# A second copy of the forget sums, batched routing, and the distance table copied from device memory

## What is computed

```python
mod = silu(c) @ w_ada                                   # six rows: shift, gain and gate, twice
h = rms_norm(x) * gain + shift
proj = h @ w_in                                         # q, k, v of "a" and of "b"; 8 forget logits a token
log_f = log_sigmoid(f_logit + b_forget)
# attention a, 8 heads of 64:  s = q.k/8 + cum[q] - cum[k], cum = cumsum(log_f); causal; softmax; @ v
# attention b, 8 heads of 64:  s = q.k/8 + rel_bias[bucket(q - k)]; causal; softmax; @ v
x = x + gate * rms_norm(concat(y_a, y_b) @ w_out)
h = rms_norm(x) * gain_f + shift_f
logits = h @ w_router + b_router                        # 32 experts
top_v, top_i = top_k(logits, 4); gates = softmax(top_v)
# every token goes to its 4 experts (swiglu, 1024 -> 2048 -> 1024), summed with the gates
```

## Time and profile before

| | |
|---|---|
| median of 3 runs | 2198.4 us (2195.64 to 2199.47) |
| the profiled execution | 2199.45 us, span 2197.5 us, mean granted clock 0.957 |
| busy: PE, weight loads, DVE, ACT, POOL | 92%, 60%, 36%, 32%, 12% of the span |
| DMA | 608.93 MB, 277 GB/s on average |
| chain that ended last | PE 70%, DMA 10%, SP queue 5%, issue 5%, DVE 5%, ACT 3% |

### The profile page before, as it was taken

One profiled execution on the slowest core, in us unless ns is written; L12 is line 12 of the kernel. 1 busy time (PEld: TensorE's weight loads), 2 busy tenths in 40 slices (PEclk: granted clock), 3 DMA queues, 4 the chain that ended last, 5 costly groups with the idle time before them and its releaser, 6 DMA issues.

```text
span 2197.5 us, 30287 instructions
## 1 busy us (share of the span) xinstructions
PE 2017.9 (92%) x11629; PEld 1311.4 (60%) x11630; DVE 800.1 (36%) x1351; ACT 704.7 (32%) x1092; POOL 260.6 (12%) x243
## 2 busy tenths in 40 slices
PE   5998699999999999999999979997999799997998
PEld 2785333333333333333333368986998699987996
DVE  2443411211111111111211166516675475246663
ACT  2434211112111221122222145523554355415543
POOL 3040000000000000000100002000242020000340
PEclk7889699999999999999999989998999899998999
DMA  9786599999896999799999855434555354453553
GB/s 356 154 285 268 232 389 418 417 416 417 325 416 284 417 416 418 324 418 416 418 418 417 362 178 178 147 118 153 170 177 191 122 192 135 135 185 122 184 182 115
DMA packets 203793, 608.93 MB, mean 277 GB/s; under 512 B 10946, under 2 KB 115542, under 8 KB 167312
## 3 DMA queue, kind: packets, MB, share of 16 engines
q1 hardware_dynamic: 197600, 585.40, 69.8%
q0 software_dynamic: 5776, 21.35, 3.4%
q10 hardware_dynamic: 328, 0.95, 0.1%
HBM read 604.51 MB, written 9.24 MB: 279 GB/s over the span
## 4 chain that ended last, share of the span: by engine, by line
PE 70%; DMA 10%; SPq 5%; issue 5%; DVE 5%; ACT 3%; DVEq 0%; ACTq 0%
PE bank L738 33%; PE bank L995 15%; PE bank L1024 9%; DMA ring<-in_w_gate_up 7%; PE bank L1088 3%; PE bank L955 2%; SPq L619 2%; SPq L622 2%; DMA ring<-in_w_in 2%; PE bank L968 1%; PE bank L988 1%; DMA ring<-in_w_ada 1%; ACT probs L1579 1%; DVE split L1416 1%; PE bank L788 1%
## 5 line engine op out<-in xcount | busy, mean ns | idle before, releaser
L995 PE MATMUL bank<-ring,qkv 128*64 128x512 f32 x2240 | 496.5, 596 | 13.4 <-DMA ring<-in_w_gate_up 13.3
L738 PE MATMUL bank<-hT_hi,split 128*128 128x256 f32 x2432 | 443.8, 285 | 5.4 <-DVE hT_lo L1424 4.0
L738 PEld LDWEIGHTS bank<-hT_hi,split 128*128 128x128 f32 x2432 | 383.4, 194 | 8.2 <-issue 6.9
L1416 DVE TENSOR_TENSOR split<-ring,split 128x2048 fp32r<-128x2048 f32 x120 | 283.8, 2367 | 265.1 <-ACT split L1737 264.9
L1737 ACT ACTIVATE split<-ring 128x2048 fp32r<-128x2048 f32 x120 | 229.6, 1913 | 415.9 <-PE bank L738 333.7
L995 PEld LDWEIGHTS bank<-ring,qkv 128*64 128x64 f32 x2240 | 155.2, 137 | 337.7 <-issue 294.4
L738 PE MATMUL bank<-hT_lo,split 128*128 128x256 f32 x1216 | 346.3, 285 | 0.0
L1024 PE MATMUL bank<-ring,qkv 128*64 128x512 f32 x1120 | 255.8, 598 | 25.7 <-ACT qkv L1698 23.5
L738 PEld LDWEIGHTS bank<-hT_lo,split 128*128 128x128 f32 x1216 | 235.8, 194 | 0.0
L1394 DVE SCALAR_TENSOR_TENSOR out_halves<-bank,probs,out_halves 64x512 fp32r<-64x512 f32 x70 | 52.5, 750 | 395.6 <-ACT out_halves L1720 395.1
L1384 DVE TENSOR_SCALAR qkv<-bank 128x512 f32<-128x512 f32 x35 | 24.2, 692 | 423.0 <-PE bank L995 423.0
(11 more groups left out here) (281 smaller groups left out, 2306.3 us busy)
## 6 DMA issues: line engine op xcount, KB each, us to landing
ring<-in_w_gate_up SPq DMA_DIRECT2D x256, 1024.0 KB, 17.0
ring<-in_w_down SPq DMA_DIRECT2D x150, 1024.0 KB, 15.8
ring<-in_w_in SPq DMA_DIRECT2D x58, 1024.0 KB, 5.4
ring<-in_w_up SPq DMA_DIRECT2D x44, 1024.0 KB, 5.1
ring<-in_w_ada SPq DMA_DIRECT2D x24, 1024.0 KB, 10.1
ring<-in_w_out SPq DMA_DIRECT2D x12, 1024.0 KB, 6.1
ring<-in_w_branch SPq DMA_DIRECT2D x12, 1024.0 KB, 5.1
neighbours<-rpb_copies POOLq DMA_DIRECT2D x32, 128.0 KB, 9.5
```

Source lines behind the costliest of these rows:

```text
L738: last = pe.matmul(out, a[a_half], b[b_half], start=start and i == 0, stop=stop and i == 2)
L995: last = pe.matmul(hidden[q][CAP * j:CAP * j + CAP, :], xgT[:, k % 4, k // 4, :], unit_at(k)[:, c:c + 512], start=False, stop=(k == KC - 1))
L1416: dve.tensor_tensor(low, unit_at(u % RING_L), high.bitcast(F32), ALU.subtract).then_inc(low_done, 1)
```

## The change

- **Forget sums.** `FOX_ROWS` is 104: the constant `fox_table` has its ones and minus ones also in rows 64 on and 96 on. `wfdup` has 64 columns and TensorE runs the product twice, to partitions 0 to 63 and 64 to 127 of the bank. The vector and scalar operations cover 104 partitions, and the product with the sums and the memset are done for rows 32 to 39 and 96 to 103. The odd head's bias takes rows 64 to 103. The wait on `odd_scores` is gone.
- **Homes.** `bada`, `trow` and `crow` move from `side` to `mixT_t`, `wfdup` to `probs_t`; two small loads of `b_forget` are added.
- **Distance table.** POOL writes the 8 rows once (`distance_rows`), waits, copies that 128 times from device memory to `distances`, and waits.
- **Routing.** Equalities, sums and gate products cover both token tiles in one instruction each; the counts are read from PSUM directly; the gates' arithmetic moves behind the evacuation of `turned`, with a bank of its own (`turned_gates`) for its transposes; the zeroing of `y_halves` moves ahead of the logits.

```diff
@@ scores
-                            if o:
-
-                                last.then_inc(odd_scores, 1)
-                                pe.wait_ge(odd_scores, tt * PAIRS + h // 2 + 1)
-                            last = extra(b, tt, h)
+                            last = extra(b, tt, h, o)
@@ TensorE, forget sums and bias
             for k in range(KC):
-                last = pe.matmul(b[0:40, 0:T], wfdup[:, k, :], hT[:, k, :], start=(k == 0), stop=(k == KC - 1))
+                for o in (0, DH):
+                    last = pe.matmul(b[o:o + DH, 0:T], wfdup[:, k, :], hT[:, k, :], start=(k == 0), stop=(k == KC - 1))
...
-            def fox_bias(b, tt, h):
-                return pe.matmul(b[:, 0:T], fcum[:, tt * P:tt * P + P], fox_rhs[:, h, :], start=False, stop=True)
+            def fox_bias(b, tt, h, o):
+                return pe.matmul(b[:, 0:T], fcum[o:o + 40, tt * P:tt * P + P], fox_rhs[o:o + 40, h, :], start=False,
+                                 stop=True)
@@ VectorE, forget sums
-            own(dve.tensor_tensor(fox_rhs[32:40], fox_rhs[32:40], fcum[32:40].unsqueeze(1).broadcast_to([8, HEADS, T]),
-                                  ALU.mult))
-            dve.memset(fcum[32:40, :], 1.0).then_inc(fox_ready, 1)
+            for group in fox_groups[1::2]:
+                own(dve.tensor_tensor(fox_rhs[group], fox_rhs[group],
+                                      fcum[group].unsqueeze(1).broadcast_to([HEADS, HEADS, T]), ALU.mult))
+            for group in fox_groups[1::2]:
+                last = dve.memset(fcum[group, :], 1.0)
+            last.then_inc(fox_ready, 1)
@@ VectorE, routing
-            for tt in range(TT):
-                for k in range(TOPK):
-                    last = dve.tensor_scalar(equal4[:, k, :], experts, bestf[:, tt, k:k + 1], None, ALU.is_equal)
-                own(last)
-                last = dve.tensor_reduce(chosen[:, tt, :], equal4.rearrange("p k e -> p e k"), AX_X, ALU.add)
...
+            own(dve.tensor_tensor(equal4, experts.unsqueeze(1).unsqueeze(1).broadcast_to([P, TT, TOPK, EXPERTS]),
+                                  over_experts(bestf[:, :, 0:TOPK]), ALU.is_equal))
+            dve.tensor_reduce(chosen, equal4.rearrange("p t k e -> p t e k"), AX_X, ALU.add).then_inc(route_ready, 1)
...
-            dve.tensor_scalar(posT, bank("turned")[0:EXPERTS, 0:T], starts, None, ALU.add)
-            leave(dve.tensor_copy(gateT, bank("turned")[0:EXPERTS, T:2 * T]), "turned")
+            leave(dve.tensor_scalar(posT, bank("turned")[0:EXPERTS, 0:T], starts, None, ALU.add), "turned")
+            dve.wait_ge(gates_exp, 1)
+            own(dve.reciprocal(gsum, gsum))
+            own(dve.tensor_tensor(gate4, gate4, gsum.unsqueeze(2).broadcast_to([P, TT, TOPK]), ALU.mult))
+            own(dve.tensor_tensor(equalg, equal4, over_experts(gate4), ALU.mult))
+            dve.tensor_reduce(gates_te, equalg.rearrange("p t k e -> p t e k"), AX_X, ALU.add).then_inc(route_ready, 1)
@@ POOL
-            pool.dma_start(distances.rearrange("q h d -> h q d"), trow.unsqueeze(1).broadcast_to([HEADS, P, 2 * T]))\
-                .then_inc(table_out, 16)
+            pool.dma_start(distance_rows, trow).then_inc(table_out, 16)
             pool.wait_ge(table_out, 16)
+            pool.dma_start(distances.rearrange("q h d -> q (h d)"),
+                           distance_rows.rearrange("h d -> (h d)").partition_broadcast(P)).then_inc(table_out, 16)
+            pool.wait_ge(table_out, 32)
```

More of the change, by code:

```diff
@@ L34 @@
 QK_SCALE = DH ** -0.5
+FOX_ROWS = DH + 40
 RING = 6
@@ L123, in shape_tables @@
     table = np.concatenate([np.asarray(a, np.float32) for a in parts.values()], 1)
[L124 to L127, removed]
+    fox = np.zeros((FOX_ROWS, HEADS, T), np.float32)
+    for base in (0, DH):
+        for h in range(HEADS):
+            fox[base + h, h], fox[base + 32 + h, h] = 1.0, -1.0
+    return np.ascontiguousarray(table), at, fox.reshape(FOX_ROWS, HEADS * T)
 class Plan:
@@ L223, in plan_first @@
         p.tile(f"g{j}")
-    for n in ("logits", "places", "counts", "ends", "turned", "list", "spread0", "spread1"):
+    for n in ("logits", "places", "counts", "ends", "turned", "list", "turned_gates", "spread0", "spread1"):
         p.tile(n)
@@ L933, in _ @@
                            stop=True))
-            read("turned")
+            pe.wait_ge(route_ready, 5)
+            b = take("turned_gates")
+            for tt in range(TT):
+                last = pe.transpose(b[0:EXPERTS, tt * P:tt * P + P], gates_te[:, tt, :], ident)
+            tile(last)
+            read("turned", "turned_gates")
             for tt in range(TT):
@@ L1247, in _ @@
             dve.wait_ge(cleared, 1)
-            for a in (0, 32):
-                last = dve.tensor_copy(wfdup[:, :, a:a + HEADS], wf)
+            for group in fox_groups[:2]:
+                last = dve.tensor_copy(wfdup[:, :, group], wf)
             last.then_inc(forget_in, 1)
@@ L1299, in _ @@
             await_own("logits")
-            for tt in range(TT):
-                own(dve.max(best[:, tt, :], logits[:, tt, :]))
-                own(dve.max_index(picked[:, 8 * tt:8 * tt + 8], best[:, tt, :], logits[:, tt, :]))
+            dve.max(best[:, 0, :], logits[:, 0, :])
+            own(dve.max(best[:, 1, :], logits[:, 1, :]))
+            dve.max_index(picked[:, 0:8], best[:, 0, :], logits[:, 0, :])
+            own(dve.max_index(picked[:, 8:16], best[:, 1, :], logits[:, 1, :]))
             own(dve.tensor_copy(bestf.rearrange("p t k -> p (t k)"), picked[:, :]))
-            for tt in range(TT):
-                last = dve.tensor_scalar(gate4[:, tt, :], best[:, tt, 0:TOPK], best[:, tt, 0:1], None, ALU.subtract)
@@ L1306, in _, with over_experts @@
-            last.then_inc(gates_in, 1)
-            for tt in range(TT):
-                for k in range(TOPK):
-                    last = dve.tensor_scalar(equal4[:, k, :], experts, bestf[:, tt, k:k + 1], None, ALU.is_equal)
-                own(last)
-                last = dve.tensor_reduce(chosen[:, tt, :], equal4.rearrange("p k e -> p e k"), AX_X, ALU.add)
-                if tt < TT - 1:
-                    own(last)
-            last.then_inc(route_ready, 1)
+            def over_experts(a):
+                return a.unsqueeze(3).broadcast_to([P, TT, TOPK, EXPERTS])
@@ L1318, in _ @@
[L1318 to L1319 removed]
+            own(dve.tensor_scalar(nblk, bank("counts")[0:EXPERTS, 0:1], float(CAP), 1.0, ALU.is_gt, ALU.add))
             for p in range(2, T // CAP):
[L1321 to L1322 removed]
+                last = dve.scalar_tensor_tensor(out=nblk, in0=bank("counts")[0:EXPERTS, 0:1], scalar=float(CAP * p),
+                                                in1=nblk, op0=ALU.is_gt, op1=ALU.add)
@@ L1323, in _ @@
                 if p < T // CAP - 1:
                     own(last)
[L1325 to L1335 removed]
+            leave(last, "counts")
@@ L1337, in _ @@
+            await_own("counts")
+            dve.tensor_copy(starts, nblk).then_inc(route_ready, 1)
             await_full("places")
```

60 lines of the change are left out of this document (26 added, 34 removed).

## The result

| | before | after |
|---|---|---|
| median | 2198.32 us (2195.64 to 2199.47) | 2180.7 us (2178.1 to 2181.82) |
| ratio, 95% interval | | 0.9919 [0.9903, 0.9935] |
| profiled execution | 2199.45 us, span 2197.5 | 2180.22 us, span 2178.5 |
| mean granted clock | 0.957 | 0.963 |

A forecast was written before the change was run, and what follows sets the result against it. Bound by device memory to 53.3 us, then TensorE, the router's VectorE chain, and DMA in the experts. +1.4 + 0.0 + 0.5 - 17.1 + 0 - 3.4 = -18.6 us gives 2180.9, forecast 2180.5; range 2175.5 to 2190.5.

The forecast's parts named there:

- 1, larger load: Loads before 53.3 us: fox_table's extra 0.52 MB makes the second weight unit land later, +1.4 us; bounds 0 and 3.1.
- 2, sums: Forget sums on TensorE: sixteen products instead of eight, halves side by side, +0.0 us; at most +3.6.
- 3, VectorE: VectorE behind the sums: second sign-table product and memset delay the next weights' low half, +0.5 us; bounds 0 and 0.6.
- 4, scores: Forget-gate scores and projections behind: two slots a pair, clock recovering after 3.0 us, -17.1 us; bounds -9.9 and -18.6.
- the rival that rested on it: Scores: each product waits for its own weight load, 6.1 us lost, giving 2187 us; chance 0.04.
- 5, distance table: Distance table copied from device memory: 0 us by itself, but keeps projection loads on time for shorter scores; bounds 0, +5.
- 6, routing: Logits to gather: batched operations, moved gates' arithmetic and earlier zeroing, 15.8 to 12.4 us, -3.4; bounds -2.2 and -4.
- (b): Routing, first product to the transposes of the places: the gates' arithmetic ahead of them moves away, -3.3 us.
- (c): Routing, transposes of the places to the spread: 2.01 us becomes 4.0 with the gates' arithmetic there, +2.0 us.
- the low clock: Scores: at most 104 of 128 rows in use, so the clock stays low; total -11.4, 2188 us; chance 0.20.
- Late weights: Late projections: POOL's earlier copies hold weight loads at 40 us, some 5 us lost, 2186 us; chance 0.06.

The follow-up runs named there:

- after_again: The changed kernel once more with no edit: 2179.65 us, ratio 0.9912 to the kernel before; its profiled execution took 2187.34 us.
- e1: The changed kernel with only fox_table loaded later, behind the addition of the token halves: 2175.55 us, one run.
- a1: The kernel before with the second copy of the forget sums and no wait, old distance table and old routing: 2193.65 us, ratio 0.9991.
- c1: The changed kernel with fox_table, three gain rows, router weights and rpb copies loaded later: 2176.28 us, ratio 0.9897, leaving out one execution of 4092.73.
- r2: The changed kernel with routing equalities, sums and gate products again one token tile after the other, gates' arithmetic still moved: 2181.34 us.
- b2: The changed kernel with three more ScalarE copies ahead of the scores, so that TensorE idles longer there: 2185.29 us, one run.
- a2: The kernel before with only the new distance copy from device memory: 2196.37 us, ratio 1.0007.
- a4: The kernel before with the second copy of the sums and the new distance copy, routing as before: 2183.54 us, ratio 0.994.
- r1: The changed kernel with the gates' arithmetic back ahead of the places on VectorE, still batched: 2171.62 us, one run.
- b1: The changed kernel with the wait between the odd head's score and bias put back, behind a lengthened gap before the scores: 2198.29 us, one run.
- a3: The kernel before with the new batched routing alone: 2194.16 us, ratio 0.9994.
- c2: The changed kernel with later small loads, plus reordered VectorE and ScalarE work to close the gap before the scores: 2174.9 us, ratio 0.9889.

## Why the prediction was right, step by step

I forecast 2180.5 us; it is 2180.7. From the profiled 2199.45 the sum gave 2180.9, and the profiled execution after took 2180.22. (One less for the median is 2179.9, so the 2180.5 that I wrote down is 0.6 more than my own sum.) The mechanisms held; that the number came this close is partly luck, as the steps show:

- **1, larger load, +1.4: held, +1.63.** The bound of 3.1, a clock that falls ahead of the second unit, was no rare case: of the eight profiled executions with the larger table in this place it fell in six, which cost 1.3 to 1.5 us more in five and 2.66 in `after_again`. What the step did not see is that the load's place was worth 3.8 us (`e1`, one execution), more than its own bytes, 2.3 us at 359 GB/s.
- **2, sums, 0.0: held,** 3.63 us for 32 instructions: the halves run side by side.
- **3, VectorE, +0.5: right in place, 0.3 short.** Second product 76.73, low half 79.80, TensorE's wait 0.58 us at 82.15; 0.82 with the restart, since the piece is split in two. My upper bound was 0.6.
- **4, scores, -17.1: the mechanism held, the size by the clock's state.** Pitch 0.87 us, no idle before the odd bias, 16 slots and the start. In the profiled execution the clock never fell and the step is 18.5, my bound of 18.6. Where it did fall the stage took 8.96 us in four kernels (`a1`, `c1`, `r2`, `after_again`), with up to 3.7 us at half clock, against my 8.8, and 10.6 in `e1`; with a longer gap (`b2`) 10.0. So the term that I took is that of the other kind of execution. The row from which I took the recovery, 3.0 us in full-array products from 118.5, came near for packed ones in those four and was half of what `b2` and `e1` needed (5.6 and 6.7 us).
- **The weight load's row against the rule.** The weight loads are again under running products of the same rows, and the slots are 0.43 us. The Trainium skill (TensorE: Matmul & The Clock Gate, Part 3, The mechanism) has it that a load overlaps only where the row group differs, though the same section also lets a load into the background weight buffer go ahead; the trace does not agree with the first, and the rival that rested on it is out.
- **5, distance table, 0 alone and the cover of step 4: held, but its price without it was not.** Write 4.6 us (I had 9), copy 8.9 (12), issued at 73.50 and landed at 82.4, no long issue on SP. `a2` shows the 0, `a4` against `a1` the cover: 10.1 us. I had put +5 as the worst; that was for a late queue, not for the old transfer under short scores, and even the expectation for `a1` was too mild. The mean share of the engines while the old transfer ran was 0.61 and is 0.90 now; the Trainium skill (DMA: Bandwidth & Descriptors, Rules for kernel authors) says that an outermost dimension of fewer than 16 entries confines a transfer to that many engines, and with 128 outermost the trace agrees: 8.9 us instead of 46.0 for the same bytes. The change also reads from device memory instead of eight partitions, and no run tells the two apart. That the old transfer also stretches the loads of others to 27 to 42 us and one issue to 25 us is what `a1` shows.
- **6, routing, -3.4: held, -3.47,** by steps -1.69, -3.45, +2.09, -0.42 against -1.5, -3.3, +2.0, -0.6. `r1` and `r2` show what the division into steps hides: (b) and (c) are one move that cancels itself but for the batching.

Of the rivals, the low clock did not come: it would have been right with the wait kept (`b1`), so the reason that I gave for it, rows in use, was not the one that decides. Late weights came only without the new distance table. The range held all eight executions of the change, 2178.1 to 2187.34 us.

Two sizes erred in opposite directions: the clock took 1.4 us more off than I took, and some 0.6 us more was lost ahead of the scores. In the medians some 2 us of the gain at the gather are not seen, within what executions differ by from gather to end.

## What to carry to other kernels

Price a part of a change together with the parts that it hides or uncovers: here one was worth at most 2 us alone, another nothing, and both together 12. A wait between small packed products costs its gap and, where the clock is down, the clock too; take it out by giving each product rows of its own, and close the gap ahead of such a stage. When VectorE's queue holds a chain of tiny operations, make them fewer and wider before you reorder them.

## What the runs showed of the hardware

- The granted clock came back under products that use 64 and 40 rows in either half in all six profiles in which it was low there, 3.6 (`a1`) to 6.7 us (`e1`) after they began. With one wait a pair it never did in four (before, `a2`, `a3`, `b1`); in `b1` it stayed at 0.50 for 18.6 us while PE showed as busy 1.90 to 1.94 of 2.00 us. In the change it also stayed at 0.50 from 241 to 256 us, with PE busy 3.00 of 3.00 us. A busy share near 1 is thus no sign that the clock will rise. What the chip counts is not settled by these runs.
- At a gap of 2.68 us the same program kept the clock in one execution and lost it in another: 7.28 or 8.96 us for the same products. Behind the other gap the same products took 5.99 us after 1.76 us of idle and 8.65 after 3.87. With a gap of 0.9 us (`c2`, one profile) it was kept.
- While a 2 MB transfer from eight partitions ran (45.8 us in `a1`), loads of 1 MB landed in 27 to 42 us, and one issue on SP's queue took 25 us; in the change the same bytes out of device memory took 8.9 us, and the loads landed in 8 to 20.
